# Expert weights of a one-core decoder step: two neighbouring rows to a partition, in half as many transfers

## The reference, cut to what matters

```
h      = rmsnorm(x, g_ff)                      # 288 x 1024
top 4 of 32 experts per token, gates = softmax over the four logits
for the tokens of expert e:
  hu   = h @ w_gate_up[e] + b_gate_up[e]       # (1024 x 2048)
  g, u = min(hu[:, :1024], 7), clip(hu[:, 1024:], -7, 7)
  a    = g * sigmoid(1.702 * g) * (u + 1)      # n x 1024
  y    = a @ w_down[e] + b_down[e]             # (1024 x 1024)
x     += sum over the four experts of gate * y
```

## Time and profile before

| | |
|---|---|
| times of three executions | 1596.06, 1601.65, 1601.97 us |
| span of the profiled execution | 1600.4 us |
| that execution's own time | not listed apart from its span |
| TensorE busy | 1477.7 us, 92% |
| VectorE, ScalarE busy | 536.5 us, 34%; 251.5 us, 16% |
| DMA queue of SP | 88.9% of 16 engines' span, 557.18 MB |
| mean granted TensorE clock | 0.953 of full speed |
| expert steps | from about 516 us to 1584 us |

### The profile page before, as it was taken

One profiled execution on the slowest core, in us unless ns is written; L12 is line 12 of the kernel. 1 busy time (PEld: TensorE's weight loads), 2 busy tenths in 40 slices (PEclk: granted clock), 3 DMA queues, 4 the chain that ended last, 5 costly groups with the idle time before them and its releaser, 6 DMA issues.

```text
span 1600.4 us, 17945 instructions
## 1 busy us (share of the span) xinstructions
PE 1477.7 (92%) x6501; PEld 616.7 (39%) x6501; DVE 536.5 (34%) x1119; ACT 251.5 (16%) x473; POOL 35.9 (2%) x39
## 2 busy tenths in 40 slices
PE   7976988998797999999999999999999999999996
PEld 4343333466545333333333333333333333333332
DVE  2049988124124222222222222222222222222224
ACT  2144443112211001110011100111001110011101
POOL 0000000004000000000000000000000000000000
PEclk9976988999995999999999999999999999999998
DMA  9976888999898999899998999999999999998980
GB/s 363 334 281 272 351 342 315 344 378 331 300 384 287 343 380 399 356 371 388 385 387 358 371 392 386 383 356 378 380 385 389 359 372 387 392 381 356 375 346 31
DMA packets 97932, 562.84 MB, mean 352 GB/s; under 512 B 12390, under 2 KB 14406, under 8 KB 58878
## 3 DMA queue, kind: packets, MB, share of 16 engines
q1 hardware_dynamic: 96565, 557.18, 88.9%
q0 software_dynamic: 1328, 5.13, 0.8%
HBM read 556.14 MB, written 73.28 MB: 393 GB/s over the span
## 4 chain that ended last, share of the span: by engine, by line
PE 88%; DVE 7%; ACT 3%; issue 1%; DMA 0%; SPq 0%; DVEq 0%
PE bank L1700 29%; PE bank L1720 14%; PE bank L1684 10%; PE bank L1646 9%; PE bank L1419 4%; PE bank L1312 3%; PE bank L1440 3%; PE bank L1526 2%; PE bank L1462 2%; DVE small L1052 2%; ACT att L863 1%; PE bank L1713 1%; DVE wide L1049 1%; PE bank L1706 1%; PE bank L1328 1%
## 5 line engine op out<-in xcount | busy, mean ns | idle before, releaser
L1700 PE MATMUL bank<-wide,att 128*64 128x512 f32 x2048 | 481.9, 602 | 0.0
L1221 DVE TENSOR_TENSOR x<-x,bank 128x512 f32<-128x512 f32 x132 | 90.8, 688 | 564.7 <-PE bank L1684 551.8
L1700 PEld LDWEIGHTS bank<-wide,att 128*64 128x64 f32 x2048 | 134.2, 136 | 312.7 <-issue 307.5
L1720 PE MATMUL bank<-slim,att 128*64 128x512 f32 x1024 | 226.8, 595 | 24.1 <-ACT att L863 24.1
L1684 PE MATMUL bank<-att 64*128 64x512 f32 (+1 forms) x384 | 176.8, 628 | 1.2 <-issue 0.7
L1646 PE MATMUL bank<-att,hn 128*128 128x128 f32 (+1 forms) x816 | 152.4, 317 | 1.9 <-DVE att L1176 1.8
L1720 PEld LDWEIGHTS bank<-slim,att 128*64 128x64 f32 x1024 | 72.5, 137 | 157.8 <-issue 154.1
L1646 PEld LDWEIGHTS bank<-att,hn 128*128 128x128 f32 (+1 forms) x816 | 115.5, 195 | 33.7 <-issue 3.1
L861 ACT ACTIVATE att<-att 128x512 f32<-128x512 f32 x32 | 20.2, 630 | 617.8 <-DVE att L1239 617.8
L1684 PEld LDWEIGHTS bank<-att 64*128 64x128 f32 (+1 forms) x384 | 42.2, 158 | 130.7 <-issue 103.0
L1225 DVE TENSOR_TENSOR x<-x,bank 32x512 f32<-32x512 f32 x66 | 44.7, 677 | 67.8 <-PE bank L1684 65.3
(11 more groups left out here) (248 smaller groups left out, 1048.1 us busy)
## 6 DMA issues: line engine op xcount, KB each, us to landing
wide<-in_w_gate_up SPq DMA_DIRECT2D x256, 1024.0 KB, 7.7
slim<-in_w_down SPq DMA_DIRECT2D x256, 512.0 KB, 6.2
out_k_win_sample<-in_cache_k_win SPq DMA_DIRECT2D x16, 2044.0 KB, 24.1
out_v_win_sample<-in_cache_v_win SPq DMA_DIRECT2D x16, 2044.0 KB, 27.8
wide<-in_cache_k_win SPq DMA_DIRECT2D x16, 1024.0 KB, 9.1
wide<-in_cache_v_win SPq DMA_DIRECT2D x16, 1024.0 KB, 6.9
wide<-in_w_in SPq DMA_DIRECT2D x8, 1024.0 KB, 13.5
wide<-in_cache_mem_k SPq DMA_DIRECT2D x8, 1024.0 KB, 19.6
```

The lines of the kernel that those rows point to most:

```text
L1221: ins = V.tensor_tensor(dst, dst, bk[:, :], ALU.add)
L1700: ins = M(bk[half[h], :], rows[:, k, :], wide[:, k, c:c + 512], start=False, stop=k == KC - 1)
L1720: ins = M(bank_y[half[h], :], aT[:, f % 4, f // 4, :], slim[:, f, 512 * h:512 * h + 512], start=f == 0, stop=f == KC - 1)
```

## The change

Both weight buffers are filled in pairs of chunks. One transfer brings 256 rows: rows 256j + 2p and 256j + 2p + 1 go to partition p, one behind the other, into chunks 2j and 2j + 1 of the buffer. The two rows are neighbours in memory, so each partition gets one run of 16384 bytes (`wide`) or 8192 bytes (`slim`), and there are four transfers of 2 MB and four of 1 MB per expert, not eight and eight. SP waits until both chunks of a pair have been used, and TensorE waits once per pair, ahead of the even chunk.

A chunk of the buffer now holds every second row of a 256-row block. The left factors of the matmuls follow: `gather` and the four transposes of `gu` read their stationary columns with a step of two (`pair_cols`), and the gain comes from a new small tile `gpair` in the same order, which four small transfers fill on SP ahead of `wr`. The four transfers have 256 elements of 4 bytes each. VectorE waits once for them. Numbers of matmuls, transposes and vector instructions don't change.

```
+        gpair = mkTf[:, 384:384 + KC]
+        def pair_cols(f):
+            return slice(256 * (f // 2) + f % 2, 256 * (f // 2) + 256, 2)
...
             load(sp, "before", before, i["c_before"])
+            for h in range(2):
+                for k in range(2):
+                    sp.dma_start(gpair[64 * h:64 * h + 64, k::2], i["g_all"][k::2, 3, h::2],
+                                 allow_slow_non_contiguous=True).then_inc(loaded["gpair"], 16)
             load(sp, "wr", wr, i["w_router"][0].rearrange("(k p) n -> p k n", p=P))
...
+            def pair_rows(name, e, j):
+                return i[name][0, e, 256 * j:256 * j + 256, :]
...   (step0 is changed in the same way)
             def step(e, n):
-                for k in range(KC):
-                    sp.wait_ge(wide_used, 8 * n + k + 1)
-                    sp.dma_start(wide[:, k, :], i["w_gate_up"][0, ds(e, 1), k * P:(k + 1) * P, :]
-                                 .rearrange("e p n -> p (e n)")).then_inc(wide_in[k], 16)
+                for j in range(KC // 2):
+                    sp.wait_ge(wide_used, 8 * n + 2 * j + 2)
+                    sp.dma_start(wide[:, 2 * j:2 * j + 2, :].rearrange("p i n -> p (i n)"),
+                                 pair_rows("w_gate_up", ds(e, 1), j).rearrange("e (p i) n -> p (e i n)", i=2)).then_inc(wide_in[2 * j], 16)
...   (slim: the same with w_down, slim_used and slim_in)
@@ evac_xe, VectorE
-                                gcol[:, 3, 4 * half:4 * half + 4].unsqueeze(2).broadcast_to([P, 4, 2 * CAP]), ALU.mult).then_inc(xe_in, 1)
+                                gpair[:, 4 * half:4 * half + 4].unsqueeze(2).broadcast_to([P, 4, 2 * CAP]), ALU.mult).then_inc(xe_in, 1)
             dve.wait_ge(parts_in, 1)
+            dve.wait_ge(loaded["gpair"], 64)
@@ gather, TensorE
-                        ins = M(bank_x[:, c:c + 2 * CAP], hn[0:m, t, P * k:P * k + P], onehot[0:m, t, :], start=t == 0, stop=t == 2)
+                        ins = M(bank_x[:, c:c + 2 * CAP], hn[0:m, t, pair_cols(k)], onehot[0:m, t, :], start=t == 0, stop=t == 2)
@@ step_, TensorE
-                    pe.wait_ge(wide_in[k], 16 * n + 32)
+                    if k % 2 == 0:
+                        pe.wait_ge(wide_in[k], 16 * n + 32)
...
-                    ins = TR(bank_t[:, P * j:P * j + P], gu[:, P * j:P * j + P], ident[:, :])
+                    ins = TR(bank_t[:, P * j:P * j + P], gu[:, pair_cols(j)], ident[:, :])
...
-                    pe.wait_ge(slim_in[f], 16 * n + 96)
+                    if f % 2 == 0:
+                        pe.wait_ge(slim_in[f], 16 * n + 96)
```

More of the change, by code:

```diff
@@ L355, in build @@
                   "state", "wpool", "pscale", "toep", "mem", "expert", "diag", "xdiag", "braw0", "braw1", "braw2", "brow", "bdn",
-                  "gfin"):
+                  "gfin", "gpair"):
             loaded[n] = sem(f"loaded_{n}")
@@ L557, in _ @@
             load(sp, "gfin", gfin, i["g_final_rows"])
+            def pair_rows(name, e, j):
+                return i[name][0, e, 256 * j:256 * j + 256, :]
             def step0():
                 sp.wait_ge(wide_used, 8)
-                for k in range(KC):
-                    sp.dma_start(wide[:, k, :], i["w_gate_up"][0, 0, k * P:(k + 1) * P, :]).then_inc(wide_in[k], 16)
+                for j in range(KC // 2):
+                    sp.dma_start(wide[:, 2 * j:2 * j + 2, :].rearrange("p i n -> p (i n)"),
+                                 pair_rows("w_gate_up", 0, j).rearrange("(p i) n -> p (i n)", i=2)).then_inc(wide_in[2 * j], 16)
@@ L564, in step0 @@
                 copy(COPIES.pop(0))
-                for k in range(KC):
-                    sp.wait_ge(slim_used, k + 1)
-                    sp.dma_start(slim[:, k, :], i["w_down"][0, 0, k * P:(k + 1) * P, :]).then_inc(slim_in[k], 16)
+                for j in range(KC // 2):
+                    sp.wait_ge(slim_used, 2 * j + 2)
+                    sp.dma_start(slim[:, 2 * j:2 * j + 2, :].rearrange("p i n -> p (i n)"),
+                                 pair_rows("w_down", 0, j).rearrange("(p i) n -> p (i n)", i=2)).then_inc(slim_in[2 * j], 16)
@@ L579, in _ @@
+                for j in range(KC // 2):
+                    sp.wait_ge(slim_used, 8 * n + 2 * j + 2)
+                    sp.dma_start(slim[:, 2 * j:2 * j + 2, :].rearrange("p i n -> p (i n)"),
+                                 pair_rows("w_down", ds(e, 1), j).rearrange("e (p i) n -> p (e i n)", i=2)).then_inc(slim_in[2 * j], 16)
             step0()
```

## The result

| | before | changed |
|---|---|---|
| median | 1599.11 us (4 executions, 1596.06 to 1601.97) | 1618.62 us (4 executions, 1617.11 to 1624.55) |
| profiled execution: time, span | span 1600.4 us | 1624.55 us, span 1622.3 us |
| mean granted TensorE clock | 0.953 | 0.946 |

The ratio is 1.0124, with a 95% interval of 1.0104 to 1.0145. The forecast was no change, 1601.3 us.

What follows compares the result with a forecast made beforehand. TensorE was taken as the bound. From the 1600.4 us span, waits took 0.3 and all other terms 0, giving 1600.1; the median's 1.25 us above the span made 1601.3 us. Range 1594 to 1630, the forecast's own 1595 to 1607.

Steps and rivals of the forecast that it cites:

- What bounds the kernel: Expert step: TensorE needs 33.31 us and is the bound; the queue's transfers need about 31.3 us, second by 2 us.
- The two queue rivals: SP's queue: larger packets free a binding queue, 1412 us, chance 0.02; larger transfers are slower, 1635 us, chance 0.02.
- Transfers in pairs, 0: Expert weight transfers: half the requests, landing after 10.2 and 8.2 us with at least 19 us to spare; value 0.
- Packets: SP's queue: 32,768 data packets less and 1024 more.
- A faster `slim` half through larger packets: `slim` transfers: may quicken, as 4096-byte packets run at 262 GB/s and 8192-byte ones at 422; value 0.
- the rival in which the queue binds: Expert transfers: the queue is the bound and larger packets free it, 6.1 us off each step, 1412 us; chance 0.02.
- Waits saved, at most 0.6 us: TensorE in the expert loop: eight waits less per step give at most 0.6 us in all; 0.3 taken.
- SP ahead of the experts, 0: SP before the expert loop: four more issues, 1.7 us, taken up by its wait for the cross-attention; value 0.
- Stationary operands with a step of two, 0: Loads of `gather` and the transposes: between 0 and 3.02 us a step more, 107 us in all at most; 0 taken.
- The granted clock: TensorE in the expert loop: read from the trace as 1.00, the upper level of 2.4 GHz.
- strided loads at a fraction of the price: Stationary loads of `gather` and the transposes: around a quarter of the full price, 27 us, gives 1628 us; chance 0.07.
- The sign named: Expert step: a load over 200 ns disproves the stride estimate, a step of more than 33.6 us the whole.

Runs made afterwards that it cites:

- e1: The changed kernel with contiguous stationary reads in `gather` and the transposes of `gu`, transfers still in pairs: 1600.37 us, ratio 1.0002 to the kernel before.
- f1: The changed kernel with the pair order made by VectorE and the load of `wr`, TensorE reading contiguously: 1599.89 us, ratio 1.0003 to the kernel before.
- s4: The changed kernel with the stationary reads of `gather` and the `gu` transposes at a step of four: 1791.58 us, ratio 1.1194 to the kernel before.
- w1: The kernel before, with one useless ScalarE copy of 64 columns ahead of its copy of the transposes: 1610.49 us, ratio 1.0061.
- w2: The kernel before, with two useless ScalarE copies of 48 columns ahead of its copy of the transposes: 1616.52 us, ratio 1.0105.
- e3: The changed kernel with `gather` contiguous, only the transposes of `gu` strided: 1609.26 us, ratio 1.0054 to the kernel before.
- e4: The changed kernel with the `gu` transposes contiguous, only `gather` strided: 1605.71 us, ratio 1.0034 to the kernel before.
- g1: The changed kernel with the last quarter of `gather` moved behind the transposes of `gu`: 1575.59 us, ratio 0.9849 to the kernel before.

## Why the prediction was wrong, point by point

The measured 1618.62 us lies inside the stated range of 1594 to 1630, but only because the range was stretched to a rival with a chance of 0.07; the forecast's own part of it, 1595 to 1607, was missed. Slower had 0.15.

- **What bounds the kernel**: right. TensorE is the bound, no matmul ever waited for a transfer, and e1 shows that changing the transfers moves nothing. The two queue rivals are out.
- **Transfers in pairs, 0**: right. They land after 9.5 and 7.2 us, where 10.2 and 8.2 had been worked out. The reserve of 19 us was never touched. The DMA share, which was to fall, didn't: f1, with these transfers and the old step, has 0.94 to 0.95 over 100 us, as before.
- **Packets**: 35,776 fewer, where 32,768 less 1024 had been named. I had left out the packets that end each transfer: 256 transfers fewer by 16 are 4096, and the four of `gpair` add 64, which gives 32,768 - 1024 + 4096 - 64 = 35,776. The pages bear the small ones out: packets under 512 bytes went from 12390 to 9381, 3009 fewer, where 4096 - 1024 - 64 = 3008.
- **A faster `slim` half through larger packets**: not seen, and the reading behind it was wrong. The 262 GB/s of the earlier trace rows are not what packets of 4096 bytes run at. In the kernel before, the same `slim` packets move 418 and 420 GB/s some microseconds later; the count of the stretch 911 to 922 us has all 911 packets under 8 KB, so no `wide` packet of 8192 bytes is among them:

```profile
918.00:920.00 2.00, 2.00 (x12) 0.61 (x10) 0.00 (x0) 1.13 (x1) 0.00 (x0) 1.00 1.02 418
920.00:922.00 2.00, 2.00 (x8) 0.44 (x4) 0.00 (x0) 0.00 (x0) 0.00 (x0) 1.00 1.03 420
DMA packets 911, 3.35 MB, mean 305 GB/s; under 512 B 92, under 2 KB 92, under 8 KB 911
```

  The low rate belongs to the first six microseconds after the queue has run dry. Twice the packet changes nothing there: (258 + 262 + 320)/3 = 280 GB/s from 912 to 918 us before, (188 + 340 + 266)/3 = 265 in the changed kernel:

```profile
918.00:920.00 2.00, 2.00 (x12) 0.67 (x10) 0.00 (x0) 0.00 (x0) 0.00 (x0) 1.00 0.69 188
920.00:922.00 2.00, 2.00 (x12) 0.72 (x10) 0.00 (x0) 0.00 (x0) 0.00 (x0) 1.00 1.05 340
922.00:924.00 2.00, 2.00 (x14) 0.77 (x12) 0.00 (x0) 1.55 (x2) 0.00 (x0) 1.00 0.77 266
```

  The batching rule of the Trainium skill ("DMA: Bandwidth & Descriptors", section "Bandwidth") didn't show here, neither in these rates nor in the time: the 0.5 MB transfers already move 418 GB/s. So the rival in which the queue binds lost its second reason too. What slows the restart of the queue wasn't tried.
- **Waits saved, at most 0.6 us**: nothing measurable (e1), in line.
- **SP ahead of the experts, 0**: right in effect. The four issues of `gpair` took 2.69 us, not 1.7, and were covered: the transfer behind the wait for `pvxt` starts at 439.64 us, against 439.63 before.
- **Stationary operands with a step of two, 0**: this is the step that failed, in two ways. First, its size: the value taken was 0, and it is 0.24 us a step, 7.7 us over the loop. The bound from above of 3.02 us held by far. The reason for 0 was that a load which isn't at one element per cycle has time to spare. It nearly holds for `gather`, whose loads take 6 ns more, but these 6 ns on 24 loads are 0.16 of the 0.24 us; it fails for the transposes, whose loads take 66 ns more. It was also drawn from the 190 ns of `gather` alone, while the transposes' loads have the same 128 columns in 140. At a step of two both end near 200 ns, as if such a load had a time of its own and the faster contiguous one lost more; that is a reading of two values, not a tested cause. The price for the gathers ahead of the loop, twice that in the loop, came out as 0: 7.57 us in both kernels. The rule of the Trainium skill ("SBUF — State Buffer", section "Specifications (TRN2)") that two hits to a line of 16 bytes are enough for full bandwidth is not what these loads show, 206 against 140 ns. Its direction is: at one hit a line (s4) `gather`'s loads take 324 ns against 196.
- **The granted clock**: second, the loop's clock was read as 1.00 and taken as given; no term and no rival of the sum let a slower load act on it. It makes 15.2 of 22.9 us in the profiled execution. w1 and w2 show that it hangs on idle or thin work between `gather` and the down matmuls by a margin of about 0.1 us a step, e3 and e4 that slower loads have the same effect as idle time, and g1 that filling the gap takes the falls away while the slow loads stay. The rival "strided loads at a fraction of the price" came nearest, with 1628 us, but by a mechanism that lacked this half.
- **The sign named** was that a load over 200 ns or a step over 33.6 us proves it wrong. The transposes' 206 ns did. A step of 33.55 us would have passed; the nine steps with a fall, at up to 35.25 us, did not.

Open is which property of TensorE's work decides on a fall; the runs vary idle time and load time, and both act alike. Open is also how many falls the executions without rows had.

## What to carry to other kernels

Before a layout is changed for the transfers' sake, look whether anything waits for them: here nothing did, so there was no gain to set against any price. Let the producer write the new order, where an engine with time to spare pays for it, and keep TensorE's stationary reads contiguous. And where a loop runs at the full clock with a repeated gap, don't count the clock as given: an addition beside the gap cost 1.2 to 3.8 times its own length here (1.2 in e4, 2.3 to 2.5 in w1, w2 and the change, 3.8 in e3, by the medians), and filling the gap was worth 2.0% by itself. And before a rate is put down to the size of packets, look at the same packets in another stretch.

## What the runs showed of the hardware

- Float32 loads of 128 stationary columns at a granted clock of 1.00: contiguous 190 ns (`gather`) and 140 ns (transposes); step of two 196 and 206; step of four 324 (`gather`).
- At 0.50 `gather`'s loads take about 320 ns, contiguous or with a step of two, and `gather` 7.57 us either way; at a step of four 324. Those of transposes take 225 ns contiguous and 217 at a step of four. No price of a step shows there.
- Packets of 4096 bytes move 418 GB/s in a full queue, and 258 to 320 in the first six microseconds after it ran dry.
- VectorE reads two float32 operands of 128x512 with a step of two in 0.69 us, as when contiguous.
- The clock went to its lower level in 0 of 32 steps with a gap of 0.76 us, in 2 with 0.88, in 6 with 0.97, and in 9 with 0.76 and strided loads. Each fall cost the 32 down matmuls 1.69 us.
